# Two transformer blocks with a 32-expert layer on one core: late division and token-half order in the first attention, norm sums in strips, router from x, another load plan for the experts' opening, sum turned a group ahead

## The chip, the core and the metric

One core of a Trainium2 chip runs the whole program. The metric is device time in microseconds (us) of one execution, the median of several. Its engines are TensorE (PE), VectorE (DVE), ScalarE (ACT), GpSimd (POOL) and SyncE (SP), which here does nothing but issue DMAs and wait. Each engine runs its own instructions in order; counting semaphores (`s_...`, and `m["..."]` in the experts) hold them together.

## What is computed

256 tokens of width 1024 pass through a first block of two layers and a second block, all in fp32:

```python
# layer 0: MLA attention (8 heads, q and k of 96, v of 64; 256 tokens + 256 ctx tokens as keys) beside a short conv
q = rmsnorm(q, q_gain); k = rmsnorm(k, k_gain)        # then rope on 32 of the 96
p = softmax(q @ k.T * QK_SCALE); a = p @ v
x = x + g1 * (concat([a, conv], -1) @ w_o)
x = x + g2 * swiglu(rmsnorm(x, norm2_g) * (1 + sc2) + sh2)      # layer 1: Fourier mixer, then the same
# second block: window attention beside an RG-LRU, then
h = rms_norm(x, g_ffn) * (1 + sc2) + sh2
logits = h @ w_router + b_router                      # top 4 of 32, softmax over the four
x = x + gt2 * sum_over_chosen(gate * expert(h))       # expert: w_gu (1024 x 2048), clipped swiglu, w_down (1024 x 1024)
out = rms_norm(x, g_final)
```

Every modulation row (sh, sc, g: 18 of 1024) is silu(c) times a 1024x1024 matrix, loaded in eight chunks of 0.5 MB (the "ada" chunks).

## The kernel before, in words

Every engine's order is written out by hand; SP's list sets the order of all loads. Activations lie with features on partitions, so a product is weights (stationary) by 256 tokens. Large dense products split each operand into a rounded high part and a remainder and take three passes (`block_product` L787 to L789: wh*ah, wh*al, wl*ah).

**First attention.** After 18 input blocks, PE makes k (`k_product` L834) by head pair, q (`q_product` L842), v (`v_product` L871). `qk_sums` sums ACT's squares over each head's 96 features: group 0 for the shared rope part of k (L851), groups 1 to 4 for k (L853), 5 to 8 for q (L857), each with 8 output columns, a row per head. The root and its reciprocal run on 8 partitions (DVE L2195), `spread` (L880) brings a head's row back to 96 partitions, where `k_norm` (L2202) applies it; two transposes (L908) turn q's factors to tokens. `v_copy` on ACT frees a bank that the last v products need; SP waits for the last of these products before it loads the blocks of w_o (L460), which ACT rounds (`block_hi`, L1459). `keep_clock` (L776) is a run of matmuls whose result nobody reads.

The loop runs 16 iterations i, head i // 2 outside, token half i % 2 inside: scores (L922: 128 tokens by 512 keys), row max on DVE (L2217, L2218), exp with row sum on ACT (L1579), reciprocal of the sum (DVE L2229), division of the 128x512 tile (ACT L1591), four transposes (L929), copy (ACT L1586), and once per head four products with v (`times_v`, L939: 64 columns of v by 256 tokens). Per chunk pair of heads ACT and DVE split the result (`ah`, `al`) for w_o. DVE also adds up 14 ada chunks meanwhile (L1957, L1958), which come into two buffers `araw`; SP may issue chunk n when chunk n - 2 is added (L449). PE's row of ada_columns (L716) closes a group of eight. Then come the w_o blocks B_O to B_F and the feed-forward (L974 to L976, L995 to L997).

**Router.** After each of eight w_out products (L1188, `out_half`) DVE forms x (L2452). ACT (L1804) and DVE (L2457) scale it by `gs` = gain times (1 + sc2) into `work`; the logits (L1231) are 16 products of that by `rout`, the norm sums (L1238) stand between them, 16 transposes (`h_turn`, L1218) make token rows, and DVE picks the top 4 and ranks the experts (L2468 to L2504); `orderi` holds the expert order, which SP needs for every dynamic load.

**Experts.** 32 experts run in 16 units of 1, 2 or 4 (unit 0 is experts 30 and 31 always, whatever the ranking). A member has eight steps of gate and up (L1327) and four of down (L1342), each with a chunk of 1 MB, 384 chunks in all. A unit's tokens are gathered by matmuls (L1300) and written to `xs` by ACT and DVE (L2600). `schedule` plans every load: which of 18 slots of 1 MB and after how many chunks read by PE. Slots 0 to 12 and 13 to 16 lie next to each other and hold 2 MB loads in eight pairs; slots 12 and 17 (17 lies split in `work` and `roots`) are `LONE_SLOTS` for two single loads whenever they are the first free. The 16 chunks of unit 0 are loaded before the order is known. At the end the last unit's result is turned (`sum_turn`, L1283) and added to x, the final norm is taken, and DVE writes x * gfin * rstd (L2626), which SP stores (L703).

The lines around the loop's order on ACT:

```python
            probs(0)
            for i in range(2 * HEADS):
                probs_divide(i)
                if i + 1 < 2 * HEADS:
                    probs(i + 1)
                probs_copy(i)
```

## Time and profile before

| | |
|---|---|
| runs | 1765.08, 1765.15, 1770.49 us; median 1765.15 |
| profiled execution | 1765.0 us, its span 1763.2 us |
| 0 to 107.7 | first modulation rows, input blocks |
| 107.7 to 154.7 | q, k, v and their norms |
| 154.7 to 205.1 | attention loop |
| 205.1 to 818.5 | w_o, feed-forward 1, Fourier, feed-forward 2, second mixer, w_out, router |
| 818.5 to 1746 | 16 expert units |
| 1746 to 1763 | last sum, final norm, stores |

A line "L716 PE MATMUL psum<-con,acc 128\*128 128x64 f32 x16" is 16 records of source line 716 on PE; an fp32 matmul leaves two records. A timeline row gives start, duration of the whole group and, in brackets, the idle time before it with what ended it. In a row of lines, busy us and mean ns are followed by the idle time before and its releaser. The granted clock (PEclk) is a share of 2.4 GHz.

### The profile page before, as it was taken

Reading aid. Unit: us, or ns where it says so; the run is one execution under the profiler, and the core shown is the slowest. Engines: PE = TensorE matmul, PEld = TensorE weight load, DVE = VectorE, ACT = ScalarE, POOL = GpSimd, SP = SyncE. Lnnn points to the kernel's source line nnn. Section 1 sums busy time; section 2 is a strip of 40 time slices with the busy share of each in tenths; the row PEclk is TensorE's granted clock in tenths of the full one; section 3 lists DMA queues with packets and bytes.
Section 4 is the critical chain, followed back from the end, with each engine's and each line's share of the span. In section 5 each row is a group of like instructions: output and inputs, shape, how many; then the busy total and the mean of one; then the engine's idle time right before and its main releaser. Section 6 shows DMA issues by size and latency. Waiting matters only on the chain.

```text
span 1763.2 us, 21693 instructions
## 1 busy us (share of the span) xinstructions
PE 1627.8 (92%) x8392; PEld 983.6 (56%) x8392; DVE 750.8 (43%) x1182; ACT 439.6 (25%) x692; POOL 125.3 (7%) x151
## 2 busy tenths in 40 slices
...
GB/s 383 225 107 167 156 238 333 297 320 177 166 256 309 324 285 271 195 89 313 400 427 426 426 426 427 426 424 427 426 426 425 425 428 417 424 426 426 427 426 206
DMA packets 80891, 586.31 MB, mean 333 GB/s; under 512 B 9856, under 2 KB 11136, under 8 KB 48544
## 3 DMA queue, kind: packets, MB, share of 16 engines
...
## 4 chain that ended last, share of the span: by engine, by line
PE 77%; DMA 15%; DVE 4%; issue 1%; SPq 1%; ACT 1%; DVEq 0%; ACTq 0%
PE psum L1327 23%; PE psum L1342 10%; DMA mraw<-dn_dram 4%; DMA mlast<-gu_dram 4%; PE psum L974 4%; PE psum L976 4%; PE psum L975 4%; PE psum L1092 3%; PE psum L1300 3%; PE psum L995 2%; PE psum L997 2%; PE psum L996 2%; PE psum L1355 2%; DMA araw<-ada_dram 2%; DMA mlast<-dn_dram 2%; PE psum L787 2%
## 5 line engine op out<-in xcount | busy, mean ns | idle before, releaser
L1327 PE MATMUL psum<-mraw,xsat 128*64 128x512 f32 (+2 forms) x1560 | 407.4, 628 | 50.7 <-DMA mraw<-gu_dram 25.9
L1327 PEld LDWEIGHTS psum<-mraw,xsat 128*64 128x64 f32 (+2 forms) x1560 | 136.6, 142 | 274.3 <-issue 273.7
L1342 PE MATMUL psum<-mraw,xsat 128*64 128x512 f32 (+2 forms) x664 | 181.1, 615 | 16.6 <-DMA mraw<-dn_dram 10.2
L1327 PE MATMUL psum<-mlast,xsat 128*64 128x512 f32 (+2 forms) x352 | 137.4, 614 | 11.7 <-DMA mraw<-gu_dram 11.7
L974 PE MATMUL psum<-wh,ah 128*128 128x512 f32 x352 | 139.4, 396 | 3.5 <-DVE al L2019 2.6
L1905 POOL TENSOR_TENSOR wl<-raw,wh 128x256 fp32r<-128x256 f32 x132 | 114.2, 902 | 366.3 <-DVE work L2046 216.8
L975 PE MATMUL psum<-wl,ah 128*128 128x512 f32 x352 | 137.3, 390 | 0.0
L976 PE MATMUL psum<-wh,al 128*128 128x512 f32 x352 | 137.3, 390 | 0.0
L2560 DVE TENSOR_TENSOR oacc<-psum,oacc 128x512 f32<-128x512 f32 x60 | 38.7, 686 | 218.0 <-PE psum L1355 218.0
L1342 PE MATMUL psum<-mlast,xsat 128*64 128x512 f32 (+2 forms) x320 | 122.0, 605 | 0.0
L2067 DVE TENSOR_TENSOR wl<-raw,wh 128x1024 fp32r<-128x1024 f32 x88 | 104.8, 1232 | 30.0 <-ACT wh L1609 29.9
L1871 ACT ACTIVATE xsat<-psum 128x512 f32<-128x512 f32 x16 | 9.6, 598 | 426.0 <-PE psum L1373 426.0
L1342 PEld LDWEIGHTS psum<-mraw,xsat 128*64 128x64 f32 (+2 forms) x664 | 58.5, 136 | 88.6 <-issue 87.0
L995 PE MATMUL psum<-mh,wh 128*128 128x256 f32 x352 | 99.9, 284 | 0.5 <-DVE ml L2265 0.5
L997 PE MATMUL psum<-mh,wl 128*128 128x256 f32 x352 | 99.6, 283 | 0.0
L996 PE MATMUL psum<-ml,wh 128*128 128x256 f32 x352 | 99.6, 283 | 0.0
L2572 DVE COPY ymo<-psum 128x512 f32<-128x512 f32 x15 | 10.4, 692 | 196.7 <-PE psum L1342 196.7
L1609 ACT ACTIVATE wh<-raw 128x2048 fp32r<-128x2048 f32 x44 | 84.1, 1912 | 15.6 <-PE psum L789 15.5
L787 PE MATMUL psum<-ah,wh 128*128 128x256 f32 (+1 forms) x272 | 81.4, 299 | 2.5 <-DVE x L2084 1.4
L788 PE MATMUL psum<-al,wh 128*128 128x256 f32 (+1 forms) x272 | 79.6, 293 | 0.0
L789 PE MATMUL psum<-ah,wl 128*128 128x256 f32 (+1 forms) x272 | 79.5, 292 | 0.0
L2590 DVE TENSOR_SCALAR work<-psum 128x1024 f32<-128x1024 f32 x16 | 19.6, 1225 | 135.3 <-PE psum L1327 135.3
...
## 6 DMA issues: line engine op xcount, KB each, us to landing
mraw<-gu_dram SPq DMA_DIRECT2D x83, 2048.0 KB, 21.8
mraw<-dn_dram SPq DMA_DIRECT2D x37, 2048.0 KB, 25.4
araw<-ada_dram SPq DMA_DIRECT2D x128, 512.0 KB, 4.8
...
mlast<-gu_dram SPq DMA_DIRECT2D x20, 2048.0 KB, 20.6
mlast<-dn_dram SPq DMA_DIRECT2D x18, 2048.0 KB, 29.3
...
raw<-ffb_dram SPq DMA_DIRECT2D x44, 512.0 KB, 5.2
```

Of the source, the lines that this page charges most:

```text
L787: mm(o, wh[:, w], ah3[:, j, 0:width], start=(j == 0), stop=False)
L974: mm(o, ah3[:, j, tok], wh[:, w], start=(j == 0), stop=False)
L975: mm(o, ah3[:, j, tok], wl[:, w], start=False, stop=False)
L976: last = mm(o, al3[:, j, tok], wh[:, w], start=False, stop=(j == DJ - 1))
L995: mm(o, wh[:, w0:w0 + P], a, start=first and j % 2 == 0, stop=False, skip_group_check=True)
L996: mm(o, wh[:, w0:w0 + P], b_, start=False, stop=False, skip_group_check=True)
L997: last = mm(o, wl[:, w0:w0 + P], a, start=False, stop=end, skip_group_check=True)
L1327: last = mm(ps[4 + n][a * w:(a + 1) * w, :], xs[:, k * P + a * w:k * P + (a + 1) * w], slot_columns(slot, n * 512), start=False, stop=(k = ...
L1342: last = mm(ps[n][a * w:(a + 1) * w, :], at[:, k * P + a * w:k * P + (a + 1) * w], slot_columns(slot, i * D + n * 512), start=(k == 0), st ...
L1609: A(wh[:, w], raw[:, w], ACT.Copy).then_inc(s_fhi, 1)
L1905: sub = lambda o, a, b: nc.gpsimd.tensor_tensor(o, a, b.bitcast(F32), ALU.subtract)
L2067: ins = TTn(wl[:, w], raw[:, w], f32(wh[:, w]), ALU.subtract)
```

## The change

1. **Norm sums in strips.** `qk_sums` goes. Head pair j writes its sums into partitions 32j to 32j+31 of the bank by four matmuls of 32 output columns: `k_sums` (4 + 4) and `q_sums` (4). The squares get four buffers, root and reciprocal run on 128 partitions, `spread` and the turn of q's factors (four tiny products with `pick4`) follow. v_product(2) and (3) come after the first four spreads.
2. **Attention.** Iteration i is token half i // 8, head i % 8. The division leaves the loop: `turn` follows exp, `times_v` runs each iteration with the probabilities stationary (four 128x64 products into [token, head dim]), `attn_scale` multiplies a half's result by the reciprocal sums, `turn_out` turns it back. B_O's conv half (12 matmuls) runs before the second `turn_out`. `pt` has four buffers.
3. **SP** issues ada(33) to ada(39) before the first feed-forward loads.
4. **Router.** `routs` = rout * gs is made once; logits come from x itself, inside the last w_out products; the scaled copies go, `h_turn` turns x, and gs is multiplied in where `xs` is made (DVE: four steps of 128x128 for one of 128x512). Three idle matmuls after h_turn for two, none before the logits.
5. **Load plan.** Unit 1's first four steps are loaded as single chunks into whatever slot is free first; the rule for lone slots goes, so slots 12 and 17 are not used after that.
6. **Last unit.** `sum_turn` before step 1 for before step 3, three idle matmuls before steps 2 and 3; x * gfin is formed ahead of the reciprocal.

The diff, cut to its core (layouts, constants and renumbered waits left out):

```diff
-PAIR_SLOTS, LONE_SLOTS = (0, 2, 4, 6, 8, 10, 13, 15), (12, SPLIT_SLOT)
-FIRST = GU_CH * len(STATIC)
+PAIR_SLOTS = (0, 2, 4, 6, 8, 10, 13, 15)
+FIRST, SINGLE_STEPS = GU_CH * len(STATIC), 4
...
+            if p == 0 and kind == "gu" and u == 1 and c < SINGLE_STEPS:
+                for a in range(len(UNITS[u])):
+                    slot = min(SLOT_ORDER, key=lambda q: free[q])
+                    load(p, (kind, u, c), a, slot, free[slot], False)
+                    free[slot] = ends[0]
+                continue
...
-                if max(free[q] for q in lone) <= max(free[q] for q in slots):
-                    slots, lone, wide = lone, LONE_SLOTS, False
...
                 ffn_a(l, 0, ffna_d[l, 0])
-                if l == 0:
-                    ada(33)
                 ffn_b(l, 0, ffnb_d[l, 0])
                 if l == 0:
-                    ada(34)
                     sp.wait_ge(s_lo, B_O + NRAW)
...
                 for j in range(6, 8):
                     ada(base_n + 40 + j)
 
+            for n in range(33, 40):
+                ada(n)
             ffn_first(0)
-            for n in range(35, 48):
+            for n in range(40, 48):
                 ada(n)
```

```diff
-            def qk_sums(u):
-                pe.wait_ge(s_qksq, u + 1)
-                if u == 0:
-                    pe.wait_ge(s_ev, B_O)
...
+            def k_sums():
+                pe.wait_ge(s_qksq, 1)
+                pe.wait_ge(s_ev, B_O)
+                for j in range(PAIRS):
+                    mm(ps[1][32 * j:32 * j + 32, :], con[NOPE:QD, _C["ones"]:_C["ones"] + 32], rt[NOPE:QD, :], start=True,
+                       stop=False, skip_group_check=True)
+                pe.wait_ge(s_qksq, 1 + PAIRS)
+                for j in range(PAIRS):
+                    last = mm(ps[1][32 * j:32 * j + 32, :], C("pair8", 32), sq[j], start=False, stop=True,
+                              skip_group_check=True)
+                last.then_inc(s_qks8, 1)
+
+            def q_sums():
+                pe.wait_ge(s_qksq, 1 + 2 * PAIRS)
+                for j in range(PAIRS):
+                    last = mm(ps[3][32 * j:32 * j + 32, :], ones[0:QD, 0:32], sq[j][0:QD], start=True, stop=True,
+                              skip_group_check=True)
                 last.then_inc(s_qks8, 1)
 
             def q_turn(j):
...
-            def times_v(h):
-                pe.wait_ge(s_ptc, 2 * h + 2)
+            def times_v(i):
+                pe.wait_ge(s_ptc, i + 1)
                 pe.wait_ge(s_vc, 4)
-                c = h // 2
-                if h % 2 == 0:
-                    wait(pe, s_aol, c - 1)
+                t, h = i // HEADS, i % HEADS
                 for k in range(4):
-                    last = mm(ps[c % 2][64 * (h % 2):64 * (h % 2) + 64, 0:T], vb[:, k, h * VD:(h + 1) * VD],
-                              pt[:, h % 2, k, :], start=(k == 0), stop=(k == 3))
+                    last = mm(ps[t][:, h * VD:(h + 1) * VD], pt[:, i % 4, k, :], vb[:, k, h * VD:(h + 1) * VD],
+                              start=(k == 0), stop=(k == 3))
                 last.then_inc(s_pv, 1)
+
+            def turn_out(t):
+                pe.wait_ge(s_dg, t + 1)
+                for c in range(4):
+                    last = nc.tensor.transpose(ps[OUT_TURN[t]][:, c * P:(c + 1) * P], sqb[:, t, c * P:(c + 1) * P], ident)
+                last.then_inc(s_psc, 1)
 
             scores(0)
...
                 if i + 2 < 2 * HEADS:
                     scores(i + 2)
                 turn(i)
-                if i % 2:
-                    if i // 2 >= 1:
-                        times_v(i // 2 - 1)
+                if i >= 1:
+                    times_v(i - 1)
                 if i == 5:
                     ada_columns(3)
-            times_v(HEADS - 1)
-
-            pe.wait_ge(s_aol, 4)
+                if i == HEADS + 5:
+                    turn_out(0)
+            times_v(TT * HEADS - 1)
             pe.wait_ge(s_csl, 4)
+            block_product(B_O, part=range(4, DJ), first=4, end=3)
+            pe.wait_ge(s_ptc, TT * HEADS)
+            turn_out(1)
+            pe.wait_ge(s_aol, TT)
             for b in range(B_O, B_F):
-                block_product(b)
+                if b == B_O:
+                    block_product(B_O, part=range(0, 4), first=4, end=3)
+                else:
+                    block_product(b)
                 if b == B_O:
                     ada_columns(4)
```

```diff
+            def logits(j):
+                pe.wait_ge(s_ev, B_XR + j + 1)
+                for t in range(TT):
+                    last = mm(ps[3][:, NEXP * t:NEXP * (t + 1)], x[:, j, t * P:(t + 1) * P], routs[:, j, :],
+                              start=(j + t == 0), stop=(j == DJ - 1), skip_group_check=True)
+                if j == DJ - 1:
+                    last.then_inc(s_lg, 1)
+
             merge_sums(0)
...
+                    pe.wait_ge(s_lruo, 5)
+                if j >= 5:
+                    for k in ((0, 1, 2), (3, 4), (5, 6, 7))[j - 5]:
+                        logits(k)
 
             def h_turn(i):
                 for k in range(4):
```

```diff
-                            if c == DN_CH - 1 and u == NU and p_ == 0:
+                            if c == 1 and u == NU and p_ == 0:
                                 pe.wait_ge(m["added"], 2 * (NU - 1))
                                 pe.wait_ge(m["at"], 2 * NU)
                                 pe.wait_ge(m["gu_read"], 2 * NU)
                                 sum_turn()
+                            if c >= 2 and u == NU and p_ == 0:
+                                keep_clock(6, 3)
                             down_product(u - 1, c)
```

```diff
+            def attn_scale(t):
+                dve.wait_ge(s_pe_, HEADS * (t + 1))
+                rows = slice(t * HEADS, (t + 1) * HEADS)
+                link(V_.reciprocal(prec[:, rows], psums[:, rows]))
+                dve.wait_ge(s_pv, HEADS * (t + 1))
+                TTn(sqb[:, t, :].rearrange("p (h d) -> p h d", h=HEADS), ps[t][:, :].rearrange("p (h d) -> p h d", h=HEADS),
+                    prec[:, rows].unsqueeze(2).to_broadcast([P, HEADS, VD]), ALU.mult).then_inc(s_dg, 1)
+
+            def attn_lo(t):
+                dve.wait_ge(s_ao, t + 1)
+                tok = slice(t * P, (t + 1) * P)
+                TTn(al3[:, 0:4, tok], ps[OUT_TURN[t]][:, :].rearrange("p (c t) -> p c t", c=4), f32(ah3[:, 0:4, tok]),
+                    ALU.subtract).then_inc(s_aol, 1)
 
```

```diff
-            def scaled(j):
-                A(work[:, j, 0:T], x[:, j, :], ACT.Copy, scale=gs[:, j:j + 1]).then_inc(s_h, 1)
-
...
-                            TTn(xs[:, 512:1024].rearrange("p (k s) -> p k s", k=4), ps[3][:, :].rearrange("p (k s) -> p k s", k=4),
-                                mod[:, 124:128].unsqueeze(2).to_broadcast([P, 4, P]), ALU.add).then_inc(m["xs"], 1)
+                            for k in range(4):
+                                ins = TS(xs[:, (4 + k) * P:(5 + k) * P], ps[3][:, k * P:(k + 1) * P], gs[:, 4 + k:5 + k],
+                                         mod[:, 124 + k:125 + k], ALU.mult, ALU.add)
...
                 STT(x[:, j, :], out_tile(j), m_col(17, j), x[:, j, :], ALU.mult, ALU.add).then_inc(s_x, 1)
+            for j in range(DJ):
+                dve.wait_ge(s_x, 2 * DJ + j + 1)
+                ins = TS(work[:, j, T:2 * T], x[:, j, :], V("gfin", j), None, ALU.mult)
+            link(ins)
             dve.wait_ge(s_rt, 7)
             link(V_.reciprocal(rstd[:, 0:T], rt[:, 0:T]))
             for j in range(DJ):
-                STT(work[:, j, 0:T], x[:, j, :], V("gfin", j), rstd[:, 0:T], ALU.mult, ALU.mult).then_inc(s_fy, 1)
+                TTn(work[:, j, 0:T], work[:, j, T:2 * T], rstd[:, 0:T], ALU.mult).then_inc(s_fy, 1)
```


On PE the norm sums stood between the products. The places from the second k product on (L834 k, L842 q, L851 to L857 sums, L863 rope turns), before:

```order
L851 MATMUL psum<-psq,con 8x512
L834 MATMUL psum<-xc,raw 128x512 x4
L853 MATMUL psum<-psq,cone 8x512
L834 MATMUL psum<-xc,raw 128x512 x2
L853 MATMUL psum<-psq,cone 8x512
L842 MATMUL psum<-xc,raw 96x256 x6
```

and in the change, from the k products to the first four spreads (L843 k, L851 q, L860 and L864 `k_sums`, L871 `q_sums`, L877 rope, L885 v, L896 spread):

```order
L843 MATMUL psum<-xc,raw 128x512 x8
L851 MATMUL psum<-xc,raw 96x256 x6
L860 MATMUL psum<-roots,con 32x512 x4
L864 MATMUL psum<-psq,cone 32x512 x2
L864 MATMUL psum<-work,cone 32x512 x2
L851 MATMUL psum<-xc,raw 96x256 x6
```

```order
L885 MATMUL psum<-raw,xc 128x512 x2
L871 MATMUL psum<-psq,con 32x512 x2
L871 MATMUL psum<-work,con 32x512 x2
L896 MATMUL psum<-roots,cone 96x512 x4
L885 MATMUL psum<-raw,xc 128x512 x4
```

Nine groups have become three, and the last two v products (L885 x4) stand behind four spreads; before, one spread stood ahead of the last of them.

In the attention loop on PE, two iterations before (L922 scores, L929 turn, L939 `times_v` once per pair):

```order
L922 MATMUL psum<-kbuf,work 128x512
L929 MATMUL psum<-con,psq 128x128 x4
L922 MATMUL psum<-kbuf,work 128x512
L929 MATMUL psum<-con,psq 128x128 x4
L939 MATMUL psum<-xc,work 64x256 x4
```

and now (L930, L937, L945), with the product in each iteration, one behind the turn:

```order
L930 MATMUL psum<-kbuf,work 128x512
L937 MATMUL psum<-con,psq 128x128 x4
L945 MATMUL psum<-work,xc 128x64 x4
L930 MATMUL psum<-kbuf,work 128x512
L937 MATMUL psum<-con,psq 128x128 x4
```

SP's dynamic loads at the experts' opening (128x4096 is 2 MB, 128x2048 1 MB, two of 128x1024 the split slot; ISA is the wait ahead of each), before:

```order
L474 DMA mraw<-gu_dram 128x4096
L472 ISA
L472 DMA work<-gu_dram 128x1024
L472 ISA
L472 DMA roots<-gu_dram 128x1024
L474 ISA
L474 DMA mlast<-gu_dram 128x4096
```

and now:

```order
L480 DMA roots<-gu_dram 128x1024
L484 ISA
L484 DMA mraw<-gu_dram 128x2048
L484 ISA
L484 DMA mraw<-gu_dram 128x2048
L484 ISA
L484 DMA mraw<-gu_dram 128x2048
```

Six single loads follow the split one where two of 2 MB stood, and the pairs begin behind them.

## Rows read from the trace of the kernel before

**Rows 1.** Busy by stretch: us, PE PEld DVE ACT POOL, clock, DMA share, GB/s.

```profile
107.70:154.70 47.00, 47.00 (x142) 19.76 (x142) 38.55 (x60) 20.25 (x33) 13.57 (x16) 1.00 0.17 56
154.70:205.10 50.40, 41.40 (x177) 21.27 (x176) 33.34 (x67) 35.37 (x69) 8.47 (x9) 1.00 0.64 219
239.30:430.00 190.70, 190.06 (x1112) 167.03 (x1116) 148.71 (x158) 92.34 (x89) 0.00 (x0) 1.00 0.79 286
860.00:1000.00 140.00, 139.84 (x620) 57.33 (x622) 28.79 (x53) 10.42 (x23) 0.00 (x0) 0.99 1.00 422
1281.00:1741.00 460.00, 379.51 (x1899) 159.60 (x1897) 78.32 (x136) 24.88 (x52) 0.00 (x0) 0.93 1.00 422
```

**Rows 2.** Timeline of PE, 104 to 155: start, duration, records.

```profile
109.60 1.02 PE L851 MATMUL psum<-psq,con 32*8 32x512 f32 x2
110.55 3.70 PE L834 MATMUL psum<-xc,raw 128*128 128x512 f32 x8
```

**Rows 3.** Timeline of PE, 1720 to 1735.

```profile
1723.14 7.07 PE L1342 MATMUL psum<-mraw,xsat 128*32 128x512 f32 x64 [0.78 <-DVE xsat L2586]
```

**Rows 4.** Timeline of the SP queue, 140 to 152.

```profile
146.81 1.28 SPq L460 DMA_DIRECT2D raw<-blk_dram  x3
```

**Rows 5.** Timeline of ACT, 146 to 160.

```profile
153.58 1.06 ACT L1459 ACTIVATE wh<-raw 128x1024 fp32r<-128x1024 f32 x1 [0.79 <-DMA raw<-blk_dram]
...
156.77 0.78 ACT L1579 ACTIVATE psq<-psum,srow,qrs 128x512 f32<-128x512 f32 x1 [0.83 <-DVE srow L2218]
```

**Rows 6.** Lines of PE and DVE, 154.7 to 205.1: busy, mean ns, idle before.

```profile
L939 PE MATMUL psum<-xc,work 128*64 128x256 f32 x64 | 14.5, 385 | 0.0
L929 PE MATMUL psum<-con,psq 128*128 128x128 f32 x64 | 10.3, 283 | 6.6 <-ACT psq L1591 6.6
...
L1958 DVE SCALAR_TENSOR_TENSOR acc<-araw,csil,acc 128x1024 f32<-128x1024 f32 x13 | 17.4, 1338 | 5.3 <-DMA araw<-ada_dram 5.3
```

**Rows 7.** Timeline of PE, 174 to 182.

```profile
174.49 2.00 PE L716 MATMUL psum<-con,acc 128*128 128x64 f32 x16
```

**Rows 8.** DMA issues, 154.7 to 205.1: count, KB, median us to landing.

```profile
araw<-ada_dram SPq DMA_DIRECT2D x14, 512.0 KB, 4.2
```

**Rows 9.** Timeline of PE, 795 to 819.

```profile
802.52 2.39 PE L1231 MATMUL psum<-xsat,work 128*128 128x32 f32 x20 [0.51 <-ACT work L1804]
...
812.13 0.47 PE L1248 MATMUL psum<-mask_,con 128*128 128x32 f32 x2
```

**Rows 10.** Timeline of DVE, 799 to 819.

```profile
806.11 0.17 DVE L2461 RECIPROCAL rsc<-rsc 128x2 f32<-128x2 f32 x1 [3.69 <-ACT rsc L1820]
808.06 0.41 DVE L2468 SCALAR_TENSOR_TENSOR logit<-psum,rsc,key 128x32 f32<-128x32 f32 x2 [1.78 <-PE psum L1231]
```

**Rows 11.** Busy time by stretch, 805 to 855.

```profile
805.00:810.00 5.00, 5.00 (x29) 5.00 (x30) 1.95 (x12) 2.62 (x5) 0.00 (x0) 0.61 1.01 418
820.00:855.00 35.00, 35.00 (x164) 13.14 (x161) 6.52 (x21) 3.68 (x8) 0.00 (x0) 1.00 0.85 327
830.00:835.00 5.00, 5.00 (x31) 2.53 (x30) 0.00 (x0) 1.14 (x4) 0.00 (x0) 1.00 0.41 151
```

**Rows 12.** Timeline of the SP queue, 785 to 890.

```profile
867.09 0.33 SPq L474 DMA_DIRECT2D mraw<-dn_dram  x1
```

**Rows 13.** Timeline of PE, 855 to 868.

```profile
862.47 4.43 PE L1327 MATMUL psum<-mraw,xsat 128*64 128x512 f32 x16
```

**Rows 14.** Timeline of PE, 1733 to 1764.

```profile
1741.36 1.07 PE L1342 MATMUL psum<-mraw,xsat 128*32 128x512 f32 x2 [4.35 <-DMA mlast<-dn_dram]
...
1742.18 1.10 PE L1342 MATMUL psum<-mraw,xsat 128*32 128x512 f32 x2
...
1744.73 0.61 PE L1342 MATMUL psum<-mraw,xsat 128*32 128x512 f32 x2
...
1745.16 0.61 PE L1342 MATMUL psum<-mraw,xsat 128*32 128x512 f32 x2
```

**Rows 15.** DMA issues, 1006 to 1012.

```profile
mraw<-gu_dram SPq DMA_DIRECT2D x2, 2048.0 KB, 15.0
```

248 lines of the change are left out of this document (111 added, 137 removed).

## Prediction, on record before the run

> **What bounds the kernel now.** I read the busy shares by stretch first, then the waits inside the stretches that the change touches, then the chain of waits, then the DMA issues. The stretches show three regimes [rows 1]. From 107.7 to 154.7 TensorE is busy for all of 47.00 us, and in the first feed-forward (239.3 to 430) for 190.06 of 190.70: such stretches pass on, one for one, whatever a stage before them gains. From 154.7 to 205.1, the first attention, it is busy 41.40 of 50.40 us, so something else decides there. Among the experts, from 860 on, DMA is full (share 1.00, 422 GB/s in both stretches shown), and from 1281 on TensorE waits for it (379.51 of 460.00 busy): the end of the experts is the end of one stream of weights. At 422 GB/s one chunk (1.049 MB by count) takes 2.48 us. The profiled execution took 1765.0 us (span 1763.2 and 1.8 around it), 0.15 below the median of the runs, so the sum holds for either.
>
> **Norm sums.** Nine small groups stand in TensorE's row, about 0.95 us each (109.60 to 110.55), a two-record matmul of 512 columns [rows 2]: 8.55 us go. Three groups of four 32-column strip matmuls come. The nearest row is the last expert's product on 32-column strips, 64 records in 7.07 us [rows 3], so 0.88 for eight records (four fp32 matmuls side by side): 2.65 us. If strips did not run side by side, twelve at 0.95 would be 11.4, and the stage longer. The TensorE row would lose 5.9, but not all of it counts: the first exp at 156.77 comes behind the block conversion at 153.58 on ACT [rows 5], whose load SP issued at 146.81 [rows 4], after v_product(3). Up to that product the row loses 8.55, gains 2.65, and gains three more spreads (0.86 each, as two-record groups) which now stand before it: -3.3 us.
>
> **The attention loop.** ACT's divide leaves each of 16 iterations. In the lines of the stretch it stands behind 6.6 us of TensorE's waits (before L929), and VectorE waits 5.3 us for the ada transfers [rows 6]. The new times_v is four 128x64 matmuls per iteration; eight of that shape took 2.00 us in ada_columns [rows 7], so about 0.95, what half of a pair's old product cost (14.5 us over 16 iterations, 0.91): no price. TensorE then needs some 0.9 (scores), 0.46 (turn) and 0.9, 2.3 us per iteration. The ada transfers land 4.2 us after issue [rows 8], and their two buffers are freed by VectorE's 1.34 us [rows 6]: (4.2 + 1.3)/2 = 2.7 us per iteration with an ada, 13 of 16. That becomes the pace, since SP now issues nine of them before the 2.5 MB of feed-forward weights. 13 x 2.7 + 3 x 2.3 = 42. Behind the last product come one scaling, four transposes, copy and subtraction, about 2.9 us with 12 of B_O's matmuls (1.4 us) beside them; I take 44.2 against 50.4: -6.2. Bounds: all waits gone, -9.0 (50.40 less 41.40); the pace as now, where only the end loses, -1. **Together -9.5, between -4 and -12.**
>
> **Router from x.** The logit matmuls (32 records, 20 of them in 2.39 us) waited 0.51 us for scaled copies [rows 9] and now stand mostly inside the product before. VectorE's logit step at 808.06 waited 1.78 us for them, with the reciprocal at 806.11 done [rows 10]; that chain is unchanged. So -1.8 to the logits, -0.2 for two dummies less: **-2.0**. Zero is the upper bound. The lower is -4: the granted clock was 0.61 from 805 to 810 [rows 11], the 1.2 GHz level for part of them, right after TensorE's 0.51 us wait and its run of tiny matmuls [rows 9]; with neither, part of the 4 us from 808.06 to the mask products at 812.13 could go at the 2.4 GHz level. "TensorE: Matmul & The Clock Gate" in the Trainium skill (Part 4) speaks against counting on it: transposes do not count as busy for the clock, and the twelve h_turn transposes still stand there. This trace does not tell them apart from the small matmuls; by the rule the router keeps its half-speed stretch, and I keep -2.0.
>
> **Load plan.** Both plans bring 16 single chunks before the order is known. Today then 4 MB can go at once and 4 MB more only after 8 and 10 chunks are read, so DMA idles: 151 GB/s from 830 to 835, and 327 instead of 422 over the 35 us from 820 to 855 [rows 11], so 8 us of stream missing. The new plan issues singles as slots come free and closes these holes: 14 MB by chunk 16, 34.7 us of stream from 820 on, so the queue would run dry near 858. But slots 12 and 17 are not used again, so 16 chunks instead of 18 can lie ahead of TensorE: at 867.09, when 18 chunks have been read, the kernel issues its 17th and 18th MB beyond those sixteen [rows 12]; the new plan its 15th and 16th only. TensorE begins unit 1 at 862.47 only [rows 13], so nothing can be issued earlier. The idle moves behind 858 and grows by 2 MB of stream: 2 x 2.48 = **+5.0** against the experts' start. Lower bound 0 (if the filled holes count), upper +7 (the latency of a load into an empty queue more: 4.2 us less 1.2 of transfer [rows 8], 3.0). "DMA: Bandwidth & Descriptors" in the Trainium skill (Measured) has 1 MB transfers at 341 GB/s against 425 at 16 MB, a rule against single loads; here the single loads of 805 to 810 ran at 418 GB/s [rows 11], so by the page eight of them would add 4.5 us (3.08 less 2.51 each), and adds nothing by the row.
>
> xs is made by four DVE steps instead of one; it stands between the first two units: **+0.35** (estimate, three more starts of some 0.1 us).
>
> **Tail.** The last products start at 1741.36 after 4.35 us of waiting, and the first group takes 0.82 us, a later one 0.43 [rows 14]; four groups run at the slower pace, 1.7 us lost at the 1.2 GHz level. keep_clock before the last two steps and the earlier sum_turn keep TensorE busy to the landing: -1.2; the cheaper last step -0.1, since SP's stores pace it. **-1.3**, between -2 and 0.
>
> **Sum:** -9.5 - 2.0 + 5.0 + 0.35 - 1.3 = -7.5: **1757.5 us**, 0.42% faster. 0.3%, or 5.3 us, is what a measurement here can tell from no change; faster means below 1759.9.
>
> **Rivals.**
> - *The opening fills its holes at no price* (the 8 us count, or TensorE frees chunks earlier than I read): no +5.0, perhaps half a microsecond more: 1752. For it: 151 GB/s in an open hole [rows 11]. Against: 867.09 [rows 12].
> - *The ada transfers pace the loop already.* VectorE's 5.3 us of waits for them [rows 6] remain, and ACT's divide was beside them: attention gives 4.5, the result is 1762.5.
> - *The clock.* Router and tail keep their 1.2 GHz stretches and the new matmuls stand in front of the last product: 0 from either: 1757.5 + 3.3 = 1760.8.
> - *Slower: the queue starves with 16 slots.* Loads issued around 1006 land 15.0 us later [rows 15]: about 3 us of latency and 12 us, some 5 MB, of queue. Two slots less leave 3 MB. It decides if TensorE lags so that under 1.2 MB (3 us) is outstanding: five holes of 2.8 us in the 281 us up to 1281 would add 14: 1771. Against it: 3 MB is still above that point.
>
> **Chances.** Forecast 0.56 (0.52 faster, 0.04 same), holes filled 0.11 (faster), loop paced 0.14 (0.02 faster, 0.12 same), clock 0.10 (0.01, 0.09), starving 0.09 (slower). Faster 0.66, same 0.25, slower 0.09. The range takes in the first four, 1752 to 1762.5 with about a microsecond at the top and half at the bottom, and leaves out the starving and some of the bounds: 1751.5 to 1763.5.
>
> **What the new profile would show.** B_O's first conv matmul near 194, the feed-forward some 9 us earlier; in the loop VectorE waiting for araw and TensorE for nothing over 0.5 us per iteration; the step from the last product to the first expert matmul 2 us shorter; DMA above 400 GB/s from 820 to 855 of today's time, then a hole of about 12 us before the first dn load; the last products at 0.43 throughout; the last landing near 1735. I am wrong if the loop keeps 3.1 us per iteration, if there is no hole after the opening, or if DMA's share drops under 0.98 in the middle of the experts.

## The result, and the profile after

The changed kernel took 1769.9 us (median of 20 runs, 1764.1 to 1775.9), the kernel before 1765.8 in the same comparison (20 runs, 1761.7 to 1770.8). The ratio is 1.0023, interval 1.0014 to 1.0031: slower, by about 4 us. The forecast was 7.5 us faster; 1769.9 lies outside its range. The profiled execution of the change took 1771.1 us, span 1769.3, 6.1 us more than the one before.

Three marks, read from the first record of each group on PE and from the landing of the last weights, tell where the time went:

| | before | changed | difference |
|---|---|---|---|
| first feed-forward matmul | 239.26 | 237.33 | -1.9 |
| first expert matmul | 818.46 | 812.72 | -5.7 |
| MB of expert weights landed at 870 | 32.1 | 32.2 | +0.1 |
| last weights landed | 1741.2 | 1748.8 | +7.6 |
| from the first product of the last step to the end | 21.8 | 20.4 | -1.4 |

The experts start 5.7 us earlier and their last weights land 7.6 us later. So 13.3 us are lost in the stream of weights, more than the rest of the change gains. (MB landed are counted in chunks of 1.049 MB, a load under way in proportion.)

**The stream.** The busy times by stretch of the changed kernel, where [rows 1] and [rows 11] show them before (us, then PE, PEld, DVE, ACT, POOL busy with counts, granted clock, DMA share, GB/s):

```profile
820.00:855.00 35.00, 32.65 (x166) 14.52 (x163) 10.48 (x23) 6.49 (x13) 0.00 (x0) 1.00 0.92 375
855.00:870.00 15.00, 14.90 (x66) 4.89 (x68) 1.91 (x11) 0.38 (x1) 0.00 (x0) 0.89 0.62 241
860.00:1000.00 140.00, 140.00 (x626) 57.52 (x624) 29.81 (x52) 11.11 (x22) 0.00 (x0) 1.00 0.99 417
1281.00:1741.00 460.00, 381.24 (x1871) 159.58 (x1872) 81.07 (x152) 27.04 (x52) 0.00 (x0) 0.91 0.99 416
1470.00:1500.00 30.00, 18.02 (x128) 5.31 (x124) 2.58 (x4) 0.00 (x0) 0.00 (x0) 0.83 0.93 386
1575.00:1610.00 35.00, 35.00 (x208) 15.15 (x207) 11.47 (x31) 3.43 (x7) 0.00 (x0) 1.00 0.84 336
```

and three of these stretches in the kernel before, which are not among its rows:

```profile
855.00:870.00 15.00, 13.23 (x73) 6.33 (x73) 6.94 (x15) 2.48 (x6) 0.00 (x0) 0.89 0.97 395
1470.00:1500.00 30.00, 20.56 (x144) 5.93 (x136) 2.58 (x4) 0.00 (x0) 0.00 (x0) 0.83 0.99 415
1575.00:1610.00 35.00, 34.14 (x182) 13.19 (x175) 8.44 (x27) 0.98 (x2) 0.00 (x0) 1.00 1.01 423
```

The holes of 820 to 855 are filled in part (375 GB/s for 327; over 400 was forecast), and the idle stands behind them, 855 to 870: one load lands at 858.70, SP issues the next at 861.88, it lands at 869.62. New are two dry places far behind, 1470 to 1500 and 1575 to 1610: 386 and 336 GB/s where 415 and 423 flowed. The SP queue of the changed kernel at the second of them:

```profile
1568.04 8.08 SPq L482 DMA_DIRECT2D mraw<-dn_dram  x2
1586.71 1.38 SPq L482 DMA_DIRECT2D mraw<-gu_dram  x3
```

The load that SP issued at 1575.78 (the second of the group at 1568.04) landed at 1585.57, and the next was issued at 1586.71: nothing was outstanding between.

**The attention.** PE's timeline of the changed kernel from the last q product to the w_o blocks, for [rows 2] and [rows 7]:

```profile
115.03 2.80 PE L851 MATMUL psum<-xc,raw 128*96 128x256 f32 x12 [0.99 <-DVE kbuf L2171]
117.76 1.06 PE L860 MATMUL psum<-roots,con 32*32 32x512 f32 x8
...
123.41 1.04 PE L877 MATMUL psum<-work,cone 32*32 32x512 f32 x2 [0.83 <-DVE work L2178]
...
139.91 1.06 PE L896 MATMUL psum<-roots,cone 32*96 32x512 f32 x2 [1.04 <-DVE work L2190]
140.90 5.40 PE L885 MATMUL psum<-raw,xc 128*128 128x512 f32 x8
...
155.92 2.07 PE L930 MATMUL psum<-kbuf,work 96*128 96x512 f32 x2 [2.90 <-ACT psq L1599]
157.79 1.06 PE L937 MATMUL psum<-con,psq 128*128 128x128 f32 x4
...
163.38 0.60 PE L937 MATMUL psum<-con,psq 128*128 128x128 f32 x4
...
196.70 1.11 PE L937 MATMUL psum<-con,psq 128*128 128x128 f32 x4 [2.48 <-ACT psq L1599]
197.61 3.51 PE L945 MATMUL psum<-work,xc 128*128 128x64 f32 x16
...
205.36 0.38 PE L795 MATMUL psum<-ah,wh 128*128 128x256 f32 x1 [1.41 <-DVE al L2240]
```

TensorE waits 0.99, 0.83 and 1.04 us, and behind the third wait eight records of v products take 5.40 us instead of the 3.70 of an equal group of k products before [rows 2]; from 141.6 the granted clock is at the 1.2 GHz level for 3.4 us. It waits 2.90 us at 153 for the first exp, and a turn takes 1.06 us (0.60 at 163.38). It waits 2.48 us at 194 for the last exp, and the last products again run slowly. In two stretches the granted clock is 0.52, nearly all of it at the 1.2 GHz level:

```profile
155.00:162.00 7.00, 6.08 (x17) 3.79 (x17) 3.77 (x7) 3.54 (x9) 7.00 (x9) 0.52 0.54 179
196.00:203.00 7.00, 6.30 (x30) 6.30 (x31) 1.49 (x3) 2.22 (x5) 0.00 (x0) 0.52 0.62 250
```

The first exp is 1.8 us earlier than at [rows 5], the first w_o load 0.5 us earlier than at [rows 4]:

```profile
152.63 1.06 ACT L1477 ACTIVATE wh<-raw 128x1024 fp32r<-128x1024 f32 x1 [0.38 <-DMA raw<-blk_dram]
...
155.00 0.78 ACT L1599 ACTIVATE psq<-psum,srow,qrs 128x512 f32<-128x512 f32 x1
```

```profile
146.33 1.28 SPq L468 DMA_DIRECT2D raw<-blk_dram  x3
```

**The router.** VectorE's row of the logits, for [rows 10], and PE's mask products, for [rows 9]:

```profile
803.68 0.17 DVE L2480 RECIPROCAL rsc<-rsc 128x2 f32<-128x2 f32 x1 [1.95 <-ACT rsc L1825]
803.95 0.41 DVE L2487 SCALAR_TENSOR_TENSOR logit<-psum,rsc,key 128x32 f32<-128x32 f32 x2
```

```profile
802.33 1.02 PE L1256 MATMUL psum<-con,work 128*128 128x1 f32 x8
803.21 1.51 PE L1249 MATMUL psum<-con,x 128*128 128x128 f32 x12
...
806.56 0.41 PE L1264 MATMUL psum<-mask_,con 128*128 128x32 f32 x2 [0.54 <-DVE mask_ L2499]
```

x is final at 801.7 in both kernels; the logits follow 4.1 us sooner (803.95 for 808.06), the mask products 5.6 us sooner, and TensorE runs at the 2.4 GHz level all through. But the feed-forward began 1.9 us earlier in the changed kernel, and x did not become final earlier. In both kernels TensorE is busy without a gap from the first w_out product behind its wait of 3.02 us to the final x, for 31.4 us before and 33.6 us now. Between the last products there now stand logit matmuls (L1212), which hold the next product back by 1.36 and 0.81 us:

```profile
793.53 1.52 PE L1212 MATMUL psum<-xsat,x 128*128 128x32 f32 x12
794.89 1.97 PE L1206 MATMUL psum<-work,mixw 128*128 128x256 f32 x8
796.70 0.97 PE L1212 MATMUL psum<-xsat,x 128*128 128x32 f32 x8
797.51 3.70 PE L1206 MATMUL psum<-work,mixw 128*128 128x256 f32 x16
```

where before they followed one another:

```profile
795.70 5.45 PE L1188 MATMUL psum<-work,mixw 128*128 128x256 f32 x24
```

### The profile page after: what moved, and what is told of

Same layout as the page of the kernel before. It is cut to its first block, busy times and chain, and to the rows that moved or that the text cites. A ratio compares the mean times of both kernels' runs of the same rounds, so it can differ in the third digit from the quotient of the medians.

```text
span 1769.3 us, 21795 instructions
## 1 busy us (share of the span) xinstructions
PE 1628.0 (92%) x8490; PEld 994.9 (56%) x8490; DVE 761.3 (43%) x1220; ACT 431.9 (24%) x668; POOL 126.6 (7%) x151
## 4 chain that ended last, share of the span: by engine, by line
PE 79%; DMA 12%; DVE 6%; SPq 2%; issue 1%; ACT 1%; DVEq 0%; ACTq 0%
PE psum L1343 24%; PE psum L1358 12%; DMA mlast<-gu_dram 5%; PE psum L992 4%; PE psum L994 4%; PE psum L993 4%; PE psum L1316 3%; DMA mlast<-dn_dram 3%; PE psum L1371 3%; PE psum L1013 2%; PE psum L1014 2%; PE psum L1015 2%; PE psum L1110 2%; PE psum L795 2%; PE psum L797 2%; PE psum L796 2%
## 5 line engine op out<-in xcount | busy, mean ns | idle before, releaser
L1343 PE MATMUL psum<-mraw,xsat 128*64 128x512 f32 (+2 forms) x1520 | 416.5, 630 | 71.1 <-DMA mlast<-gu_dram 65.0
L1343 PEld LDWEIGHTS psum<-mraw,xsat 128*64 128x64 f32 (+2 forms) x1520 | 138.4, 142 | 327.0 <-issue 325.5
L1343 PE MATMUL psum<-mlast,xsat 128*64 128x512 f32 (+2 forms) x520 | 242.6, 629 | 0.0
L1358 PE MATMUL psum<-mraw,xsat 128*64 128x512 f32 (+2 forms) x816 | 223.4, 611 | 10.0 <-DMA mlast<-dn_dram 9.1
L1358 PEld LDWEIGHTS psum<-mraw,xsat 128*64 128x64 f32 (+2 forms) x816 | 75.5, 141 | 134.6 <-issue 132.5
L1358 PE MATMUL psum<-mlast,xsat 128*64 128x512 f32 (+2 forms) x208 | 96.3, 616 | 0.0
L1343 PEld LDWEIGHTS psum<-mlast,xsat 128*64 128x64 f32 (+2 forms) x520 | 71.2, 144 | 32.6 <-issue 32.4
```

The costliest lines, as they stand in the source:

```text
L1343: last = mm(ps[4 + n][a * w:(a + 1) * w, :], xs[:, k * P + a * w:k * P + (a + 1) * w], slot_columns(slot, n * 512), start=False, stop=(k = ...
L1358: last = mm(ps[n][a * w:(a + 1) * w, :], at[:, k * P + a * w:k * P + (a + 1) * w], slot_columns(slot, i * D + n * 512), start=(k == 0), st ...
```

## The experiments

Three rounds each; the ratio is to the kernel before in the same set of runs (e1 to e4, e5 to e8 and e9 to e12 are sets). "Landed at 870" and "last landing" are counted from the landing times of all expert loads in the profiled execution. The last column is the time from the first expert matmul to the last landing: it tells of the stream alone, whatever the front did in that execution. It is 922.8 us in the kernel before and 936.0 in the changed one.

| run | median us | ratio to before, interval | first expert | landed at 870, MB | last landing | stream, us |
|---|---|---|---|---|---|---|
| e1 old plan in the change | 1758.5 | 0.9950 (0.9930 to 0.9969) | 811.1 | 34.3 | 1734.7 | 923.5 |
| e2 singles, 18 slots | 1763.4 | 0.9985 (0.9973 to 0.9996) | 812.9 | 32.1 | 1740.6 | 927.7 |
| e3 new plan alone | 1775.7 | 1.0044 (1.0028 to 1.0060) | 820.2 | 30.0 | 1751.9 | 931.7 |
| e4 router alone | 1763.4 | 0.9982 (0.9972 to 0.9991) | 821.0 | 30.8 | 1744.2 | 923.2 |
| e5 twelve single steps, 18 slots | 1756.9 | 0.9954 (0.9941 to 0.9966) | 810.7 | 36.4 | 1732.8 | 922.1 |
| e6 e5 + idle matmuls | 1753.5 | 0.9935 (0.9919 to 0.9952) | 809.0 | 37.2 | 1731.5 | 922.5 |
| e7 e5 + last ada steps later | 1752.8 | 0.9931 (0.9914 to 0.9948) | 807.4 | 37.6 | 1730.1 | 922.7 |
| e8 attention alone | 1762.6 | 0.9980 (0.9971 to 0.9990) | 820.5 | 31.2 | 1741.9 | 921.4 |
| e9 e6 and e7 | 1753.4 | 0.9926 (0.9909 to 0.9943) | 812.1 | 36.8 | 1732.6 | 920.5 |
| e10 e9 + spread moved | 1751.4 | 0.9916 (0.9899 to 0.9933) | 808.6 | 37.3 | 1730.5 | 921.9 |
| e11 e9, old last unit | 1754.0 | 0.9932 (0.9915 to 0.9948) | 811.0 | 36.3 | 1732.8 | 921.8 |
| e12 e9, old plan | 1756.3 | 0.9950 (0.9934 to 0.9967) | 809.3 | 35.0 | 1732.7 | 923.4 |

### The load plan: e1, e2, e3, e5, e12

**e1** puts the schedule of before into the changed kernel:

```diff
-PAIR_SLOTS = (0, 2, 4, 6, 8, 10, 13, 15)
+PAIR_SLOTS, LONE_SLOTS = (0, 2, 4, 6, 8, 10, 13, 15), (12, SPLIT_SLOT)
...
-            if p == 0 and kind == "gu" and u == 1 and c < SINGLE_STEPS:
...
+                if max(free[q] for q in lone) <= max(free[q] for q in slots):
+                    slots, lone, wide = lone, LONE_SLOTS, False
```

> The changed kernel with the load plan of before (18 slots, 2 MB loads in the opening), everything else changed. Theory A (the new load plan costs, once for the two slots that are no longer used and once for a queue that runs dry at units 12 to 14): first expert matmul near 812.7 as in the changed kernel, last weights landing near 1735.5 (the landing of before, 1741.2, less the 5.7 us by which the experts start earlier) against 1748.8, run about 1757.5. Theory B (the transfers before the experts or the longer last unit set the end, the plan does not matter): last landing above 1741, run above 1763.

1758.5 us, 11.4 less than the changed kernel, last landing 1734.7: theory A, and B falls. The new plan turns a faster kernel into a slower one.

**e2** keeps the singles and puts only the rule for the lone slots back:

```diff
+    lone = LONE_SLOTS
...
+                if max(free[q] for q in lone) <= max(free[q] for q in slots):
+                    slots, lone, wide = lone, LONE_SLOTS, False
```

> The changed kernel with the single loads of the opening kept, and the rule for the two lone slots (12 and 17) put back behind them. Theory A: what costs is the loss of two slots, not the singles: last landing 1733 to 1736, run 1755 to 1758, equal to the run with the old plan within 2 us or better. Theory C (single loads themselves cost in the opening): 3 us or more slower than the run with the old plan.

1763.4: 6.5 us better than the change, 4.9 worse than e1. The late places are healed, the opening is not:

```profile
855.00:870.00 15.00, 14.76 (x66) 4.74 (x68) 2.04 (x11) 0.38 (x1) 0.00 (x0) 0.89 0.62 242
1470.00:1500.00 30.00, 20.00 (x140) 5.80 (x136) 2.58 (x4) 0.00 (x0) 0.00 (x0) 0.83 1.00 422
1575.00:1610.00 35.00, 33.00 (x174) 12.85 (x167) 8.04 (x30) 0.98 (x2) 0.00 (x0) 1.00 1.01 423
```

So the two slots are the whole of the loss at 1470 to 1610 (422 and 423 GB/s again), and not the cause of the one at 855 to 870 (242 GB/s). Theory A was wrong in that half, and theory C, as it was worded, is met by the number; but its reason (single loads as such) is not what the plan shows. Counted in the plan (`schedule` run for each kernel), as MB that may be issued ahead of those that PE has read:

| chunks read by PE | 0 | 4 | 8 | 12 | 16 | 20 | 24 | highest behind 24 | 204 | 264 | 308 |
|---|---|---|---|---|---|---|---|---|---|---|---|
| before, e1, e12 | 17 | 16 | 14 | 16 | 16 | 18 | 18 | 18 | 15 | 14 | 14 |
| changed, e3 | 18 | 18 | 16 | 14 | 14 | 14 | 16 | 16 | 12 | 12 | 12 |
| e2 | 18 | 18 | 16 | 14 | 14 | 14 | 18 | 18 | 15 | 14 | 14 |
| e5 | 18 | 18 | 18 | 18 | 18 | 18 | 16 | 18 | 15 | 14 | 14 |

Singles placed in whatever slot is free first take one half of a pair and leave the other half idle for the 2 MB loads behind them. Until chunk 22 these halves are lost, in e2 as in the change, and TensorE pauses between unit 0 and unit 1 just there. The columns 264 and 308 are the two late places, in the units of four: two MB less at points that are the narrowest anyway. A low number alone is not enough: the changed plan is down to 12 MB at sixteen counts, 204 among them, and the landings show marked losses at these two places only.

**e5** follows from that: all twelve steps of the opening single, in 18 slots.

```diff
-            if p == 0 and kind == "gu" and u == 1 and c < SINGLE_STEPS:
+            if p == 0 and (kind == "gu" and u == 1 or kind == "dn" and u == 0):
```

> The changed kernel with all twelve steps of the opening (gate-up of unit 1, down of unit 0) as single 1 MB loads into any of 18 slots, the rule for slots 12 and 17 put back behind them. Theory A2 (what the opening loses is slots that lie idle because half of a pair is still unread, so the number of MB that may be issued ahead decides): 18 MB ahead at every count up to 22, the stream never dry, 36.0 MB landed at 870 us (34.3 with the old plan, 32.2 with the changed one), last landing near 1730, run near 1754. Theory B2 (34 MB at 870 is what the queue can do, or single loads are slower): no better than 1758.

1756.9, 6.5 us below e2; the stream no longer stops:

```profile
820.00:855.00 35.00, 32.55 (x166) 14.54 (x162) 12.38 (x32) 6.29 (x13) 0.00 (x0) 0.97 1.01 422
855.00:870.00 15.00, 15.00 (x70) 4.78 (x68) 0.00 (x0) 0.00 (x0) 0.00 (x0) 0.95 1.00 394
```

36.4 MB had landed at 870 (36.0 by theory A2); the last landing, 1732.8, is 3 us later than expected, since of the 4.3 MB of lead over e2 3.5 are left at 1700: near 1007, where a 2 MB load was issued only at 999.13, three MB take 10.0 us to land, 2.7 more than in full flow. Against e1 the whole is worth only 1.6 us, across two sets and within the intervals, so it was measured again in one set and with one front.

**e12** is e9 (below) with the plan of before.

```diff
-            if p == 0 and (kind == "gu" and u == 1 or kind == "dn" and u == 0):
-                for a in range(len(UNITS[u])):
...
-    lone = LONE_SLOTS
+    lone = SLOT_ORDER[FIRST:]
```

> e9 with the load plan of before in place of the twelve single steps, so that both are compared on one chip with the same front. Theory A2 (18 MB ahead at every count of the opening): about 36.5 MB against 34.5 landed 60 us behind the experts' start, e12 slower than e9 by 3 to 5 us. If the singles give nothing against the old plan: within 1 us.

1756.3 against 1753.4: 2.9 us, intervals that still overlap by a little; the stream takes 923.4 us against 920.5. The sign is that of A2, the size just under the 3 to 5 us expected.

**e3** is the converse, the new plan in the kernel before.

```diff
+            if p == 0 and kind == "gu" and u == 1 and c < SINGLE_STEPS:
...
-                if max(free[q] for q in lone) <= max(free[q] for q in slots):
-                    slots, lone, wide = lone, LONE_SLOTS, False
```

> The kernel of before with the new load plan alone. Theory A: 5.0 us from the opening and 7.7 us from the dry queue at units 12 to 14, last landing near 1754, run about 1778. Theory B: no more than 3 us slower than before. If the opening's filled holes counted (a rival of the prediction) it would be faster than before.

9.6 us slower in the medians, 7.8 by the ratio (interval 4.9 to 10.6). Last landing 1751.9, 10.7 later than before; the late dry places are there too (389 GB/s from 1470 to 1500, 345 from 1575 to 1610). The two losses of theory A are both seen. Its first expert matmul came 1.8 us later than in the kernel before; counted from there the stream is 8.9 us longer, where theory A had 12.7. Why the opening cost less here than in the changed kernel was not followed up.

### The front: e8, e6, e7, e9, e10

**e8** is the attention part alone (strips, loop, order of the ada loads) in the kernel before.

```diff
-            k_product(0)
-            qk_sums(0)
...
-            for i in range(2 * HEADS):
-                probs_divide(i)
...
+            for n in range(33, 40):
+                ada(n)
             ffn_first(0)
```

> The kernel of before with the attention part alone (strips, token halves, late division, order of the ada loads). The changed kernel began its feed-forward 1.9 us earlier, so by the traces this is worth 1.9 us: run 1764, feed-forward 1.9 us earlier. By the prediction 9.5.

1762.6, 3.0 us less in the medians (interval of the ratio 1.8 to 5.1 us). The feed-forward of its profiled execution begins at 240.46, later than before's 239.26: this one execution (1765.8 us) is the slowest of its ten, with both half-clock stretches of the attention longer (10.2 us each). One execution does not measure 2 us here. Five profiled executions have this attention (changed, e1, e2, e5, e8) and three the old one (before, e3, e4). From the first k product to the feed-forward they take 127.5 to 133.3 us, mean 129.4, against 131.5 to 132.9, mean 132.4: 3.0 us less, as in e8's medians, with a spread that is larger than the gain.

**e6** puts idle matmuls ahead of TensorE's two long waits (bank 0, free at both places), on e5:

```diff
             scores(1)
+            keep_clock(6, 0)
...
+                if i == 2 * HEADS - 1:
+                    keep_clock(5, 0)
                 turn(i)
```

> e5 with six idle matmuls behind the first two score products and five ahead of the last turn, where TensorE had waited 2.90 and 2.48 us in the changed kernel and then ran at half the clock (155 to 162 and 196 to 203 us). Theory H (part of what the attention failed to gain is the half clock that follows these two waits): granted clock 1.00 in both stretches, feed-forward 3 to 4 us earlier, run 3 us faster than e5. Theory D (the loop is paced by the ada transfers, the clock is beside the point): feed-forward less than 1 us earlier.

**e7** instead lets the last two ada steps of the loop follow the last row max:

```diff
-                if i < 5 or 6 <= i < 14:
+                if i < 5 or 6 <= i < 12:
                     ada(27 + i if i < 5 else 26 + i)
+                if i >= 14:
+                    ada(24 + i)
```

> e5 with the last two ada steps of VectorE's loop moved behind the last row max, so that no row max stands behind a wait for a transfer at the end. Theory D: the 1.93 us wait for araw, the 2.48 us wait of TensorE for the last exp and the half clock behind it go, feed-forward 3 to 5 us earlier. Theory H: the wait goes but the end hangs on the scaling and turning of the second half; less than 1.5 us.

Feed-forward at 231.77 and 231.86 (e5: 235.01), run 3.3 and 4.1 us below e5: theory H is met by e6 and theory D by e7, each with its own edit. In e6 no stretch of the loop has the half clock, in e7 one from 154 to 164 still has it. In e7 VectorE's last row max no longer stands behind a transfer, and TensorE goes from the last turn to w_o without a wait (the 1.41 us ahead of B_O's other half are as in the change):

```profile
191.01 0.69 DVE L2229 TENSOR_REDUCE srow<-psum 128x1 f32<-128x512 f32 x1 [1.25 <-PE psum L933]
...
194.06 1.28 DVE L1967 SCALAR_TENSOR_TENSOR acc<-araw,csil,acc 128x1024 f32<-128x1024 f32 x1 [0.91 <-DMA araw<-ada_dram]
```

```profile
193.81 0.61 PE L940 MATMUL psum<-con,psq 128*128 128x128 f32 x4
194.25 1.96 PE L948 MATMUL psum<-work,xc 128*128 128x64 f32 x16
...
199.53 0.39 PE L798 MATMUL psum<-ah,wh 128*128 128x256 f32 x1 [1.41 <-DVE al L2243]
```

In the changed kernel the same row max (194.81) had come behind a 1.93 us wait for araw:

```profile
193.61 1.28 DVE L1964 SCALAR_TENSOR_TENSOR acc<-araw,csil,acc 128x1024 f32<-128x1024 f32 x1 [1.93 <-DMA araw<-ada_dram]
194.81 0.68 DVE L2226 TENSOR_REDUCE srow<-psum 128x1 f32<-128x512 f32 x1
```

**e9** has both.

```diff
+            keep_clock(6, 0)
...
-                if i < 5 or 6 <= i < 14:
+                if i < 5 or 6 <= i < 12:
```

> e5 with both attention edits: idle matmuls ahead of the two waits (e6) and the last two ada steps behind the last row max (e7). In e7 TensorE still ran at half the clock from 154 to 164 us, in e6 it still waited for the last exp. If the start belongs to the clock and the end to the ada wait, the two gains add up in part: 2 to 4 us below e7 (1752.8), near 1750. If both removed the same wait: 1752 to 1753.

1753.4, no better than either: by its own criterion both remove the same wait, and what e6 gains at the start cannot be told from the scatter (the feed-forward is at 230.98, 0.9 us earlier than in e7). Its profiled execution also shows what else the clock does. From 805 to 812, in the router, TensorE ran at the 1.2 GHz level, and its step from feed-forward to experts is 5.6 us longer than e7's (581.1 against 575.6): 2.7 of them stand there and 3.0 in w_out. That second place is a common one: behind a wait of 3.0 us for a norm, some 50 us ahead of the experts, nine of the fourteen profiled executions fell to 1.2 GHz for 3.4 or 6.8 us (e2, e3, e4, e6, e8 to e12), and before, changed, e1, e5 and e7 did not. First e4, then the kernel before:

```profile
770.00:775.00 5.00, 4.26 (x10) 3.50 (x11) 4.31 (x10) 3.78 (x9) 0.00 (x0) 0.50 0.04 16
```

```profile
770.00:775.00 5.00, 4.73 (x22) 4.21 (x23) 3.88 (x9) 3.32 (x8) 0.00 (x0) 1.00 0.01 5
```

**e10** moves the fourth spread, which had waited 1.04 us, behind v_product(2):

```diff
-            for n in range(PAIRS):
+            for n in range(PAIRS - 1):
                 spread(n)
             v_product(2)
+            spread(PAIRS - 1)
             v_product(3)
```

> e9 with the fourth spread moved behind v_product(2); in the changed kernel it waited 1.04 us for VectorE's rope and the four v products behind it ran at half the clock (141.6 to 145), which held back SP's load of the w_o blocks and with it the first exp. If the strips' gain was lost there: load issued 2 to 3 us earlier, run 2 us below e9. If the first exp hangs on something else (the table load, the k norms): within 0.5 us of e9.

The wait of 1.04 us is gone (0.23 us are left, for ACT), SP issues the w_o blocks at 144.53 (145.49 in e9, 146.33 in the change) and the first exp starts at 153.22 (154.86 in e9, 155.00 in the change). Only e9 differs by this edit alone: 1.0 us for the load and 1.6 for the exp, where 2 to 3 us for the load were expected. The rest of the 1.8 us against the change is the half clock from 141.6 on: with one and the same code it stood there in the change, e2, e6, e8, e11 and e12 (39.3 to 39.4 us from the first k product to the load) and not in e1, e5, e7 and e9 (37.7). In all ten executions and in e10 the exp follows the load by 8.4 to 9.4 us, so it does hang on that chain:

```profile
144.53 1.28 SPq L471 DMA_DIRECT2D raw<-blk_dram  x3
```

```profile
153.22 0.78 ACT L1606 ACTIVATE psq<-psum,srow,qrs 128x512 f32<-128x512 f32 x1
```

1751.4 us, 2.0 below e9; the intervals overlap. It is the fastest version of the study: 13.6 us below the kernel before (0.84% by the ratio) and some 18 below the changed one.

### Router and last unit: e4, e11

**e4** has the router part alone, in the kernel before.

```diff
-            def scaled(j):
-                A(work[:, j, 0:T], x[:, j, :], ACT.Copy, scale=gs[:, j:j + 1]).then_inc(s_h, 1)
...
+                if j >= 5:
+                    for k in ((0, 1, 2), (3, 4), (5, 6, 7))[j - 5]:
+                        logits(k)
```

> The kernel of before with the router part alone (logits from x, gs multiplied in where xs is made). The changed kernel began its feed-forward 1.9 us and its experts 5.7 us earlier, so the router should be worth 3.8 us: first expert matmul near 814.7, run about 1761.5. If only the 2.0 us of the prediction belong to it, 816.5 and 1763.3. If the time to the experts' start is given back by loads that do not move with it, the run stays at that of before.

1763.4 (ratio interval 1.6 to 4.9 us faster). It fits 3.8 and 2.0 alike. Its profiled execution (1769.0, the slowest of ten) is the one with the half clock at 770 above, and it ran at the 1.2 GHz level in the router as well, for 6.8 us from 814.4 on; feed-forward to experts took 581.3 us, more than with the old router in e8 (580.0, with the same 6.8 us in w_out and 3.4 in the router). The 3.8 us are read from the changed kernel, where feed-forward to experts is 575.4 us, before 579.2 (575.4 to 577.2 in e1, e2, e5, e6 and e7).

**e11** is e9 with the last unit and the last step of before.

```diff
-                            if c == 1 and u == NU and p_ == 0:
+                            if c == DN_CH - 1 and u == NU and p_ == 0:
...
-                            if c >= 2 and u == NU and p_ == 0:
-                                keep_clock(6, 3)
```

> e9 with the last unit and the last step as before (sum_turn ahead of step 3, no idle matmuls, scalar_tensor_tensor at the end). The changed kernel took 20.4 us from the first product of the last step to the end of the span, before 21.8: 1.4 us slower than e9.

0.6 us slower in the medians, which is within the scatter. In the two profiled executions the time from last landing to the end is 22.8 against 20.8 us; over all profiled executions it is 22.0 to 23.0 in the five with the old last unit and 20.5 to 20.8 in the nine with the new one. The gain is seen there, not in the runs.

## Why the prediction was wrong

Two steps of the sum failed. The attention was to give 9.5 us and gave 1.9 (3.0 by e8's medians): the sum had TensorE's list and a pace of the ada transfers in it, and no wait and no half clock. The queue behind the opening had no term at all: it ran low at two places and once dry, and lost 10.0 us, of which 2.2 came back elsewhere. The other terms together miss by about 2 us, most of it the router's, to the good.

**Norm sums: right in price, wrong in what follows.** Four strip matmuls take 1.0 us (117.76 to 118.75), forecast 0.88; they do run side by side. But the step "-3.3 us" up to v_product(3) counted PE's instructions and left out their waits. With the sums gathered behind the products, TensorE waits 0.99, 0.83 and 1.04 us for copies and rope where it had stood busy for 47 us [rows 1], and the v products then run at 1.2 GHz (5.40 us for 3.70). The w_o load came 0.5 us earlier, not 3.3, and the first k product already 0.8 earlier (106.95 for 107.73): from there to the load nothing was gained (39.4 us for 39.1). Without the half clock, in e1, e5, e7 and e9, it is 37.7, a gain of 1.4: the forecast's 3.3, less 2.9 us of waits, less 0.3 for dearer strips, plus 1.2 because the spreads cost less than 0.86 each (six records in 1.22), come to 1.3. The reading of [rows 5] left out a wait: ahead of that exp stand 0.83 us of waiting for VectorE's row max, so before it was the row max that came last and not the conversion; in the change the conversion and the table load come last. The strips without the new loop were not run.

**Attention loop: the step that fixed its pace failed.** "13 x 2.7 + 3 x 2.3 = 42": the ada transfers do not set the pace in the middle. From 163 to 182 one iteration follows another every 2.19 us but for one ada_columns group of 1.95, TensorE busy. (By its own terms the sum is 42 + 2.9 = 44.9, not 44.2.) They count at two places. Behind the first token half TensorE waits 1.18 us for an exp (185.34) whose row max stands behind a wait of 1.27 us for araw and the scaling:

```profile
181.41 1.28 DVE L1964 SCALAR_TENSOR_TENSOR acc<-araw,csil,acc 128x1024 f32<-128x1024 f32 x1 [1.27 <-DMA araw<-ada_dram]
```

```profile
185.34 1.12 PE L930 MATMUL psum<-kbuf,work 96*128 96x512 f32 x2 [1.18 <-ACT psq L1599]
```

And at the end VectorE's row max of the last iteration stands behind the wait for a chunk, TensorE waits for the exp, and the half clock makes the tail of the stage longer (197.61, 3.51 us; 1.96 in e7). At the start the first exp comes 3.9 us behind its scores. Neither a wait nor a clock stretch had a term in the sum. Together the attention gave 1.9 us in the profile, 3.0 in e8's medians, not 9.5. With the last ada steps moved (e7), and with the idle matmuls and the moved spread besides (e10), the feed-forward begins 7.4 and 8.8 us earlier than before: most of the 9.5 was there, but not in this order of instructions. The rival "the ada transfers pace the loop already" was nearer in size (4.5) and had the culprit nearly right, and its mechanism wrong.

**Router: right in sign, two terms wrong.** -3.8 for -2.0, from the feed-forward to the first expert. "That chain is unchanged" was a failing step: the norm sums (L1238) stood behind 20 records of logit matmuls on PE, so the reciprocal moved as well, from 806.11 to 803.68. From the final x to the first expert matmul it is 11.0 us for 16.8, so 5.8 are gained. That the logits "now stand mostly inside the product before" was priced at nothing: there TensorE is busy throughout, and the final x comes 2.2 us later for it. Much of the 5.8 is clock: idle matmuls and transposes ran at 2.4 GHz (twelve transposes 1.51 us, before 2.80), so the mask products waited 0.54 us only. In e3 and e8 the old router had 3.4 us at the 1.2 GHz level for the 6.8 of before, and took 15.2 us. Against these the new one gains 15.2 - 11.0 - 2.2 = 2.0, the forecast's number, by luck. "TensorE: Matmul & The Clock Gate" in the Trainium skill (Part 4), by which the transposes do not keep the clock up, would have left the half clock in place. In nine of the eleven profiled executions of the new router it stayed at 2.4 GHz through twelve of them, with matmuls before and behind (11.0 us); in e4 and e9 it fell for 6.8 us behind them (13.7 us). Whether the transposes counted cannot be told from that.

**Load plan, opening: right in size, not in reason.** +5.0 against the experts' start was forecast; 32.2 MB landed at 870 in the change and 34.3 in e1 are 2.1 MB, or 5.2 us (1.6 of them because e1's experts began earlier), and e2's stream is 4.9 us longer than before's. The queue ran dry at 858.7, near the 858 of the forecast. But the reason given, the two unused slots, is refuted by e2: it may use them and loses as much. By the plan's numbers it is idle halves of pairs, and e5, in which they do not lie idle, has 36.4 MB. "DMA: Bandwidth & Descriptors" in the Trainium skill (Measured) puts a 1 MB transfer at 341 GB/s; the queued singles of e5 ran at 422 from 820 to 855, with several outstanding. The trace does not agree; that measurement is of another issuing engine, GpSimd, and here SP issues.

**Load plan, later: the rival that decided.** "The queue starves with 16 slots" had 0.09, because the fewest MB outstanding were looked for near 1006 only ("3 MB is still above that point"). This is the failing step. The place is behind the units of four (1470 to 1500, 1575 to 1610), where loads were issued with 2 MB outstanding and once with none. Counted in landings, the change is 1.0 MB ahead of before at 1400 (246.9 for 245.9) and 2.8 behind at 1700 (364.6 for 367.4), and its last landing is 7.6 us later: 10.0 us are lost there, and e2, with before's landings from 870 to the end, shows that the two slots are the cause. What the change gains from 870 to 1400, 0.9 MB or 2.2 us, goes with the two slots too, since e2 does not have it (246.0 MB at 1400). That single and split loads are dearer (about 2.5 us per MB where a 2 MB load takes 2.45) fits this, but was not tested by itself. The rival's 1771 lies near the measured 1769.9 by luck: its 14 us for the holes came on top of a front that had gained all 9.5.

**DVE's four steps for xs:** they take 1.36 us where the one step took 0.68, twice the forecast's 0.35 more:

```profile
853.68 1.36 DVE L2620 TENSOR_SCALAR xsat<-psum,gs,mod 128x128 f32<-128x128 f32 x4
```

The lead of the experts falls by 0.68 there (5.74 to 5.06), and is 5.20 us once both kernels are past the half clock behind that wait. **Last unit:** -1.4 for -1.3 in the profile; the last products run at 2.4 GHz (0.43 apart, 1748.92 to 1749.37 and on):

```profile
1745.92 2.86 PE L783 MATMUL psum<-con 128*128 128x256 f32 x12
...
1748.92 1.00 PE L1358 MATMUL psum<-mraw,xsat 128*32 128x512 f32 x3
```

By the profile the terms then close: -5.2 (lead of the experts behind unit 0) + 5.0 (opening) - 2.2 (870 to 1400) + 10.0 (dry queue) = +7.6 for the last landing; less 1.4 in the last unit is +6.2, the spans differ by 6.1. The medians differ by 4.1: a span scatters by some microseconds, and where TensorE falls to 1.2 GHz differs between executions.
